# Two attentions of a hybrid decoder layer as flat sequences of steps, with their projections dealt out between the steps; input norm and latents in one block

## The chip, the core and the metric

The kernel runs on one core of a Trainium2 chip. TensorE (PE in the rows) multiplies, VectorE (DVE) and ScalarE (ACT) do elementwise work, GpSimd (POOL) makes masks and issues indirect transfers, SyncE (SP) issues most transfers. The engines run side by side and wait for each other through semaphores. The metric is the device time in microseconds (us) of one launch, median of several runs; lower is better.

## The reference

One decoder layer for 1024 tokens of width 1024, all in float32. What matters here is the mixer part:

```python
h = rmsnorm(x, norm_mix)
q_a, kv_a, dq, dk, dv, gates = split(h @ w_in)
# first mixer (MLA): 8 heads, query and key of 64 + 32 (rotary), value of 64
q = rmsnorm(q_a) @ w_q_b;  kv = rmsnorm(c_kv) @ w_kv_b      # latents of rank 256 and 128
p = softmax(causal(q_nope @ k_nope + q_rope @ k_rope) * scale);  y_mla = p @ v_mla
# second mixer (differential): 4 heads, two queries and two keys of 64 each, value of 128
p0, p1 = softmax(causal(q_c @ k_c * scale + bias[t5_bucket]))  for c in (0, 1)
y_diff = rmsnorm((p0 - lam * p1) @ v_d) * (1 - lambda_init)
x = x + (sigmoid(g_mla) * (y_mla @ w_up_mla) + sigmoid(g_diff) * (y_diff @ w_up_diff)) @ w_out
x = x + moe_ffn(rmsnorm(x))          # top 4 of 32 experts
```

After it comes the final norm. The experts take more than half of the time and are not touched.

## The kernel before

The program is a row of blocks (`nc.Block`). Inside a block each engine has its own list of instructions and meets the others by semaphores; at the end of a block all engines meet. The blocks are `stage_norm`, `stage_latents`, `stage_mla`, `stage_diff`, `stage_merge`, `stage_out`, `stage_route`, `stage_experts`. The change touches the first four.

- `stage_norm` (L230): x comes in 8 tiles of 128 tokens through four buffers. ScalarE sums squares and takes the root (L273, L276), VectorE scales (L296, L298), TensorE transposes (L288), VectorE applies the gain while it moves the tile out of PSUM into `ht` (L306), which holds h transposed. VectorE starts when all five gain vectors have landed (L268).
- `stage_latents` (L310): SyncE and ScalarE issue the loads of weights and small tables at its start. TensorE makes three latent tiles of 128 channels (L403), sums their squares with a matrix of ones (L415), makes the rotary key and the same with halves swapped (L422: two passes of 32 columns), then eight value tiles of the second mixer (L432, 8 products each), eight of the first (L438), and turns the bias table (L443). VectorE meanwhile makes the arguments of sine and cosine, one reciprocal of 2048 columns (L496), and moves the value tiles out of PSUM (L511).
- `stage_mla` (L640): a loop over four pairs of heads. A pass begins with the pair's projections (L684: rotary and plain queries, 8 products of 512 columns; L688: keys, 2 products), which VectorE and ScalarE move to SBUF (L753 to L757, L807, L810). Then come 16 steps, one for each head and tile of 128 queries. A step on TensorE is `score` (L700) of the next step, `turn` (L713, transposes of the probabilities) of this one, `apply` (L724, probabilities times values) of the one before. VectorE adds the mask and takes the row maximum (L768, L770), ScalarE does the exponential (L816); both copy the turned probabilities (L777, L822); VectorE scales the result (L782, L784). Query tile i sees i + 1 key tiles, so steps grow with i from 0 to 7.
- `stage_diff` (L854): a loop over four heads. A pass begins with 32 products of 512 columns (L893), copied by ScalarE (L1024) and VectorE (L961). Then come 8 steps with two score halves each (L908), bias and maximum (L973, L976), exponential (L1031), `combine` (L981 to L987), `turn` (L920), copies (L994, L1044), `apply` (L930), result and its squares (L998, L1037). Each score half has one pair of PSUM banks: `score` of the next step waits for the exponential of this one.

`either` (L530) reads a flag that tells whether positions are one apart, and each engine then takes one of two versions of the work; with these inputs it is the short, causal one. Instructions in a loop pass are written once; in the projections of a float32 product one `matmul` leaves two MATMUL records.

## Time and profile before

| | us |
|---|---|
| median of 3 runs | 2996.05 |
| lowest, highest | 2992.53, 2996.17 |
| time of the profiled execution | 3004.51 |
| its span | 3003.0 |
| granted TensorE clock over the span | 0.95 of full speed |
| TensorE busy | 2808.7 (94%) |
| VectorE busy | 1480.1 (49%) |
| ScalarE busy | 1033.4 (34%) |

The profiled execution takes 8.5 us more than the median. The time falls into stretches: input norm to 28.9 us, latents 29.4 to 186, first mixer 191 to 462, second mixer 469 to 761, merge to 1063, output projection, norm and routing to about 1264, experts to the end. In a row of a timeline the first number is the start and the second the length; what stands in brackets is how long the engine sat idle before and who released it. In a row of a table by stretches the first number after the stretch is its length, then busy time and instructions of each engine, then the granted clock of TensorE (1.00 is 2.4 GHz, 0.50 is 1.2 GHz), share and rate of the transfers.

### The profile page before, as it was taken

How to read it: one execution, taken by the hardware profiler on the slowest of the kernel's cores; microseconds unless marked ns; L12 is line 12 of the kernel's file. 1: busy time of each engine (PE TensorE's matmuls, PEld its weight loads, DVE VectorE, ACT ScalarE, POOL GpSimd, SP SyncE). 2: the span in 40 equal slices, each digit the busy share in tenths (PEclk: the TensorE clock that was granted, in tenths of full speed). 3: DMA queues.
4: the chain of work that ended last, by engine and by line, in shares of the span. 5: the costliest groups of instructions: out<-in, count | busy, mean ns of one | idle time of the engine just before them, and what ended most of it. 6: DMA issues, size and time to landing. Idle time of an engine off the chain costs nothing.

```text
span 3003.0 us, 47092 instructions
## 1 busy us (share of the span) xinstructions
PE 2808.7 (94%) x16548; PEld 2275.4 (76%) x16549; DVE 1480.1 (49%) x2566; ACT 1033.4 (34%) x1610; POOL 293.7 (10%) x308
## 2 busy tenths in 40 slices
PE   6988888888899999799999999999999999999995
PEld 3346664544566645489999999999899999999995
DVE  4334443444411114666666666666345554444554
ACT  2013332222311012145555555554233333333333
POOL 0000000000000012301111111111111111111111
PEclk9988888889999999599999999999999999999997
DMA  4000001000211153566676766666899999999995
GB/s 129 0 10 5 4 0 29 14 14 0 63 42 42 42 180 50 184 202 195 205 222 210 220 198 218 201 216 217 265 338 344 338 339 342 341 341 343 346 337 179
DMA packets 425339, 522.88 MB, mean 174 GB/s; under 512 B 29428, under 2 KB 336280, under 8 KB 425256
## 3 DMA queue, kind: packets, MB, share of 16 engines
q1 hardware_dynamic: 402504, 464.05, 47.6%
q0 software_dynamic: 18432, 57.20, 7.8%
q10 hardware_dynamic: 4352, 0.98, 0.2%
q8 instruction: 29, 0.48, 0.1%
q14 instruction: 22, 0.18, 0.0%
HBM read 482.23 MB, written 39.95 MB: 174 GB/s over the span
## 4 chain that ended last, share of the span: by engine, by line
PE 56%; issue 0%; DMA 0%; DVE 0%; ACT 0%; SPq 0%; POOLq 0%; POOL 0%; ACTq 0%
PE banks L1814 20%; PE banks L1824 19%; PE banks L1865 16%; PE banks L1806 1%; DVE arena L2108 0%; DMA arena<-acc_rows 0%; DMA acc_rows<-arena,rows 0%; ACT parts L1909 0%; DVE parts L2029 0%; SPq L1746 0%; ACT arena L2001 0%; ACT parts L1936 0%; ACT arena L1980 0%; DVE stat L2106 0%; POOLq L1772 0%
## 5 line engine op out<-in xcount | busy, mean ns | idle before, releaser
L1814 PEld LDWEIGHTS banks<-arena 128*128 128x128 f32 x5376 | 604.9, 192 | 8.2 <-issue 6.6
L1814 PE MATMUL banks<-arena 128*128 128x128 f32 x5376 | 605.2, 275 | 6.2 <-issue 6.2
L1824 PE MATMUL banks<-parts 128*128 128x256 f32 x4608 | 558.0, 284 | 7.1 <-issue 4.0
L1824 PEld LDWEIGHTS banks<-parts 128*128 128x128 f32 x4608 | 557.3, 193 | 8.7 <-issue 4.4
L1865 PE MATMUL banks<-parts 128*128 128x512 f32 x2160 | 498.3, 391 | 0.0
L1865 PEld LDWEIGHTS banks<-parts 128*128 128x128 f32 x2160 | 403.0, 188 | 82.1
L2025 DVE TENSOR_TENSOR parts<-arena,parts 128x1024 fp32r<-128x1024 f32 x264 | 315.3, 1222 | 128.3 <-ACT parts L1929 127.8
L2048 DVE TENSOR_SCALAR arena<-banks,arena 128x128 f32<-128x128 f32 (+1 forms) x528 | 181.4, 393 | 335.4 <-PE banks L1814 335.4
L2029 DVE TENSOR_TENSOR parts<-arena,parts 128x1024 fp32r<-128x1024 f32 x192 | 233.8, 1223 | 197.0 <-ACT parts L1936 195.7
L1929 ACT ACTIVATE parts<-arena 128x1024 fp32r<-128x1024 f32 x264 | 269.7, 1054 | 88.4 <-PE banks L1865 44.9
L1936 ACT ACTIVATE parts<-arena 128x1024 fp32r<-128x1024 f32 x192 | 201.1, 1053 | 178.0 <-PE banks L1824 117.7
L1136 PE MATMUL banks<-parts 128*128 128x512 f32 x768 | 184.3, 399 | 4.3 <-ACT parts L1156 4.3
L1136 PEld LDWEIGHTS banks<-parts 128*128 128x128 f32 x768 | 145.1, 189 | 41.5 <-issue 12.2
L1957 ACT ACTIVATE parts<-arena 128x256 fp32r<-128x256 f32 (+1 forms) x132 | 65.4, 496 | 260.3 <-DVE arena L2056 255.4
L1953 ACT ACTIVATE arena<-arena 128x256 f32<-128x256 f32 (+1 forms) x132 | 65.3, 495 | 235.9 <-DVE arena L2048 235.9
L1332 PE MATMUL banks<-arena 128*128 128x512 f32 x256 | 115.2, 609 | 6.2 <-PEq L1086 3.2
L893 PE MATMUL banks<-arena,arena 128*128 128x512 f32 x256 | 112.6, 601 | 7.4 <-issue 7.4
L1791 POOL COPY rows<-entries 128x2 int32 x33 | 5.9, 177 | 1156.3 <-ACT arena L1980 1156.3
L1766 POOL DMA_INDIRECT acc_rows<-arena,rows x66 | 109.3, 1657 | 66.2 <-issue 66.2
L1211 DVE TENSOR_TENSOR arena<-banks,arena 128x512 f32<-128x512 f32 x32 | 20.6, 686 | 189.8 <-ACT arena L1167 189.8
L1128 PE MATMUL banks<-arena 128*128 128x512 f32 x256 | 112.5, 592 | 1.5 <-DVE arena L1191 1.5
L893 PEld LDWEIGHTS banks<-arena,arena 128*128 128x128 f32 x256 | 49.1, 193 | 68.0 <-issue 68.0
(287 smaller groups left out, 2674.4 us busy)
## 6 DMA issues: line engine op xcount, KB each, us to landing
arena<-in_w SPq DMA_DIRECT2D x264, 1024.0 KB, 7.6
arena<-in_w SPq DMA_DIRECT2D x66, 2048.0 KB, 12.7
arena<-in_w_in SPq DMA_DIRECT2D x27, 512.0 KB, 5.0
arena<-in_x SPq DMA_DIRECT2D x16, 512.0 KB, 4.4
h_rows<-arena POOLq DMA_DIRECT2D x10, 512.0 KB, 7.5
acc_rows<-arena SPq DMA_DIRECT2D x8, 512.0 KB, 4.3
arena<-acc_rows SPq DMA_DIRECT2D x8, 512.0 KB, 7.7
out<-arena SPq DMA_DIRECT2D x8, 512.0 KB, 5.7
```

The lines of the kernel that those rows point to most:

```text
L893: last = nc.tensor.matmul(bank(g, 2 * s + c), wst[:, s, k, :], ht[:, k, c * HALF:(c + 1) * HALF], start=(k == 0), stop=(k == KT - 1))
L1128: nc.tensor.matmul(bank(g, 4 * h + b), w[s][b][:, k, :], yt[:, k0 + k, cols], start=(k == 0), stop=(k == 3))
L1136: last = nc.tensor.matmul(bank(g, 4 * h + b), w_parts[:, s, c, b, k, :], part[:, k, cols], start=(k == 0 and c == 0 and part is h_hi), sto ...
L1332: last = nc.tensor.matmul(bank(g, 2 * (t % 2) + h), merged[:, k, t * P:(t + 1) * P], w_out[:, k, h * HALF:(h + 1) * HALF], start=(k == 0), ...
L1814: last = nc.tensor.matmul(bank(g, 2 * (c % 2) + s)[:, a * JOB:a * JOB + P], w1[c][:, s, k, a * P:(a + 1) * P], xt[:, k, 0:P], start=(k == ...
L1824: last = nc.tensor.matmul(bank(g, 2 * (c % 2) + s)[:, a * JOB:(a + 1) * JOB], first_part[p][:, y, k, :], x[:, k, :], start=(k == 0 and y = ...
L1865: last = nc.tensor.matmul(bank(g, 2 * c + h), x[:, f, rows], second_part(q, wide)[:, y, a, :], start=(f == 0 and x is act_hi and y == 0), ...
L1929: nc.scalar.activation(second_part(q, wide)[:, 0], piece_of(q), ACT.Copy).then_inc(w_hi_ready, 1)
L1936: nc.scalar.activation(first_part[p][:, 0], first_of(p), ACT.Copy).then_inc(v_hi_ready.sem, 1)
L2025: nc.vector.tensor_tensor(part[:, 1], piece_of(q), part[:, 0], ALU.subtract).then_inc(w_lo_ready, 1)
L2029: nc.vector.tensor_tensor(first_part[p][:, 1], first_of(p), first_part[p][:, 0], ALU.subtract).then_inc(v_lo_ready.sem, 1)
L2048: nc.vector.tensor_scalar(dst[:, a, 0:w], bank(g, 2 * (c % 2) + s)[:, a * JOB:a * JOB + w], b1_t[:, bass.ds(expert, 1), s * FT + 2 * c + a ...
```

## The change

`stage_norm` and `stage_latents` become one block, `stage_front`. x gets a buffer for each tile; the gain vectors other than `norm_mix` and the small tables move to GpSimd's queue; weights are issued right behind x. The products of the first latent tile's first half stand between the last three transposes. The rotary key and its swapped form are one pass of 64 columns (16 products for 32). Three value tiles of the second mixer are made there (`DV_EARLY`); five are left.

`stage_mla` has no loop over pairs: 128 steps in a row. `side_plan` deals out "units" between `score` and `turn`: the next pair's projections as six units (rotary, plain, keys, for each half of the tokens) in the steps of the pair's second head, and the five value tiles, 3 + 3 + 2 products in the first three steps of each pair (and once more in the last). All of them use PSUM bank 7, so `apply` has bank 6 alone. A unit's first product waits until the unit before it is out of the bank (`wait_taken`); VectorE takes rotary units, ScalarE the others. The results go to a second set of buffers.

`stage_diff` has no loop over heads: 32 steps. A unit is one 512-token half of a head's keys or queries, 8 products in bank 7. Two units stand ahead; the others follow at 4 products a step (8 in step 0), up to step 26. ScalarE copies a unit as fp32r (`high`: 4 copies for keys, 2 for queries), VectorE subtracts that copy from the product to get the rest (`low`, two instructions), and only then does the bank come free. The scores are two fp32r products in place of one float32 product: high and low part of the query stacked on 128 rows times the high key, and high query times low key on 64 rows.

```diff
 def stage_front(g, io):
...
+            for t in range(5):
+                turn(t)
+            pe.wait_ge(w_ready[0], 16)
+            for t, ks in ((5, range(0, 3)), (6, range(3, 6)), (7, range(6, 8))):
+                turn(t)
+                latent(0, 0, ks)
+            pe.wait_ge(ht_ready, TT)
+            latent(0, 1, range(KT)).then_inc(projected, 1)
...
-            for swapped, b in ((0, 6), (1, 4)):
-                for h in range(2):
-                    for k in range(KT):
-                        last = nc.tensor.matmul(bank(g, b + h)[NOPE:HEAD_QK, :], wst[:, 3, k, swapped * ROPE:(swapped + 1) * ROPE],
+            for h in range(2):
+                for k in range(KT):
+                    last = nc.tensor.matmul(bank(g, 6 + h)[NOPE:P, :], wst[:, 3, k, 0:2 * ROPE],
...
 def stage_mla(g, io):
...
-                with pe.Fori(0, MLA_HEADS // 2) as hp:
...
+                    for n, k in fill[u]:
+                        side(n, k)
+                    if u == MLA_STEPS - 1:
+                        apply(u - 1)
+                    turn(u)
...
+                def wait_taken(n):
+
+                    pe.wait_ge(rot_steps, 2 * rotated(n))
+                    pe.wait_ge(side_taken, n - rotated(n))
...
 def stage_diff(g, io):
...
+                    if k == 0:
+                        pe.wait_ge(g.w_head[h % 3], 64 if h == 3 else 32)
+                        if n >= ahead:
+                            pe.wait_ge(lo_made, n)
...
-                                last = nc.tensor.matmul(bank(g, 2 * c + a // HALF)[:, 0:n], q_t[rows, i * P:(i + 1) * P],
-                                                        k_t[rows, a:a + n], start=True, stop=True)
+                        nc.tensor.matmul(out, q_c[c][:, cols], k_c[h % 2][c][:, a:a + n], start=True, stop=False)
+                        last = nc.tensor.matmul(out, q_c[c][rows, cols], k_low[h % 2][rows, a:a + n], start=False, stop=True)
...
+                    half = len(fill[u]) // 2
+                    if u + 1 < DIFF_STEPS:
+                        score(u + 1, 0)
+                    for n, k in fill[u][:half]:
+                        project(n, k)
+                    if u + 1 < DIFF_STEPS:
+                        score(u + 1, 1)
+                    for n, k in fill[u][half:]:
+                        project(n, k)
...
+                    if kind == KEY:
+                        k0, k1 = k_c[h % 2]
+                        for out, rows in ((k0[first, cols], first), (k0[second, cols], first), (k1[second, cols], second), (k1[first, cols], second)):
+                            last = nc.scalar.activation(out, src[rows], ACT.Copy)
+                    else:
+                        for c0, rows in ((0, first), (1, second)):
+                            last = nc.scalar.activation(q_c[c0][rows, cols], src[rows], ACT.Copy, scale=DIFF_SCALE)
+                    last.then_inc(hi_made, 1)
```

Where instructions stand now, on TensorE from the latents' rotary key on. Before (L415 sums of squares of the last latent, L422 rotary key, L432 value tiles of the second mixer, L438 of the first, L443 bias):

```order
L415 MATMUL banks<-arena_0,ones 128x512 x2
L422 MATMUL banks<-arena_0,arena_1 32x512 x32
L432 MATMUL banks<-arena_0 128x512 x64
L438 MATMUL banks<-arena_1 128x512 x8
L443 MATMUL banks<-arena_1,flip 128x256 x4
```

After (L387, L393, L401, L409, L414 are the same five):

```order
L387 MATMUL banks<-arena_0,ones 128x512 x2
L393 MATMUL banks<-arena_0,arena_2 64x512 x16
L401 MATMUL banks<-arena_1,arena_0 128x512 x24
L409 MATMUL banks<-arena_1,arena_2 128x512 x8
L414 MATMUL banks<-arena_1,flip 128x256 x4
```

Of 96 products of these two kinds 40 are left. TensorE around the start of a pair's second head in the first mixer, after the change (L740 is `score`, L724 a rotary unit, L753 `turn`, L764 `apply`):

```order
L740 MATMUL banks<-arena_1 128x256
L724 MATMUL banks<-arena_0 128x512 x2
L753 MATMUL banks<-ident,arena_0 128x128
L764 MATMUL banks<-arena_0 128x64 x8
L740 MATMUL banks<-arena_1 128x384
L724 MATMUL banks<-arena_0 128x512 x2
L753 MATMUL banks<-ident,arena_0 128x128 x2
L764 MATMUL banks<-arena_0 128x64
```

The rotary units of the next pair stand in steps whose own work is small. Before, the same eight products of both query kinds stood in a row ahead of the pair's first score (L684, keys L688, `score` L700):

```order
L684 MATMUL banks<-arena_0 128x512 x8
L688 MATMUL banks<-arena_1,arena_0 128x512 x2
L690 ISA
L691 ISA
L700 MATMUL banks<-arena_1 128x128
L700 MATMUL banks<-arena_1 128x256
```

TensorE in the second mixer, before: a whole head's projections, then its first steps (L908 `score`, L920 `turn`):

```order
L893 MATMUL banks<-arena_0,arena_1 128x512 x32
L896 REGISTER_ALU
L908 MATMUL banks<-arena_1 128x128 x2
L904 REGISTER_ALU
L908 MATMUL banks<-arena_1 128x256
L904 REGISTER_ALU
L908 MATMUL banks<-arena_1 128x256
L913 ISA
L920 MATMUL banks<-ident,arena_0 128x128
```

After, one step in the middle of a head (L1021 and L1022 are the two fp32r products of a score half, L1005 the unit's products, L1034 `turn`, L1045 `apply`):

```order
L1021 MATMUL banks<-parts_3 128x512
L1022 MATMUL banks<-parts_3 128x512
L1021 MATMUL banks<-parts_3 128x128
L1022 MATMUL banks<-parts_3 128x128
L1005 MATMUL banks<-arena_0,arena_1 128x512 x2
L1021 MATMUL banks<-parts_3 128x512
L1022 MATMUL banks<-parts_3 128x512
L1021 MATMUL banks<-parts_3 128x128
L1022 MATMUL banks<-parts_3 128x128
L1005 MATMUL banks<-arena_0,arena_1 128x512 x2
L1034 MATMUL banks<-ident,arena_0 128x128 x4
L1045 MATMUL banks<-arena_1,arena_0 128x128 x3
```

Each half of the scores is followed by two products of a unit, and each projection waits in TensorE's queue for its bank. On ScalarE the copies of a unit come after the step's probabilities are copied (L1185 exponential, L1199 copy of turned probabilities, L1174 `high` of keys, L1192 squares):

```order
L1185 ACTIVATE arena_0,den<-banks,den 128x768 x2
L1199 ACTIVATE arena_0<-banks 128x512
L1174 ACTIVATE parts_3<-banks 64x512 x4
L1192 ACTIVATE arena_0,ssq<-arena_1 128x128
L1185 ACTIVATE arena_0,den<-banks,den 128x896 x2
```

Before, ScalarE had one copy of 1024 columns for a head's queries (L1024), ahead of the steps.

## Rows read from the trace of the kernel before

**Rows 1.** The page, chain that ended last: shares of the span by line.

```profile
PE banks L1814 20%; PE banks L1824 19%; PE banks L1865 16%; PE banks L1806 1%; DVE arena L2108 0%; DMA arena<-acc_rows 0%; DMA acc_rows<-arena,rows 0%; ACT parts L1909 0%; DVE parts L2029 0%; SPq L1746 0%; ACT arena L2001 0%; ACT parts L1936 0%; ACT arena L1980 0%; DVE stat L2106 0%; POOLq L1772 0%
```

**Rows 2.** Table by stretches: length, busy us of each engine, clock, transfers.

```profile
33.30:48.70 15.40, 15.40 (x33) 6.61 (x33) 4.74 (x6) 0.00 (x0) 0.00 (x0) 0.90 0.97 254
48.70:91.20 42.50, 35.79 (x79) 14.87 (x78) 17.81 (x22) 3.26 (x6) 0.00 (x0) 0.96 0.06 18
91.20:118.80 27.60, 27.60 (x65) 6.96 (x64) 16.45 (x4) 5.50 (x5) 0.00 (x0) 1.00 0.00 1
118.80:182.70 63.90, 63.81 (x153) 28.80 (x152) 15.47 (x21) 0.00 (x0) 0.00 (x0) 1.00 0.03 5
182.70:191.00 8.30, 0.00 (x0) 0.00 (x0) 2.89 (x6) 1.28 (x1) 1.04 (x4) 0.73 0.02 6
191.00:205.30 14.30, 11.66 (x20) 4.80 (x20) 4.88 (x4) 4.08 (x4) 0.00 (x0) 0.80 0.05 9
205.30:260.00 54.70, 49.40 (x264) 37.88 (x265) 26.18 (x70) 21.24 (x49) 0.00 (x0) 0.83 0.03 5
260.00:329.00 69.00, 61.10 (x287) 42.91 (x287) 31.60 (x77) 25.31 (x53) 0.00 (x0) 0.82 0.03 5
469.20:500.30 31.10, 29.71 (x64) 12.86 (x65) 1.23 (x1) 1.02 (x1) 0.00 (x0) 0.94 0.01 2
617.00:690.00 73.00, 63.72 (x225) 35.39 (x224) 32.70 (x70) 20.62 (x59) 0.00 (x0) 0.91 0.06 14
```

**Rows 3.** Groups by line: value tiles (float32), merge products (fp32r); two and one record each.

```profile
L1136 PE MATMUL banks<-parts 128*128 128x512 f32 x768 | 184.3, 399 | 4.3 <-ACT parts L1156 4.3
...
L432 PE MATMUL banks<-arena 128*128 128x512 f32 x128 | 55.2, 593 | 0.0
```

**Rows 4.** Timeline of the norm's first and last tile and the first latent.

```profile
10.42 0.16 DVE L296 RECIPROCAL stat<-stat 128x1 f32<-128x1 f32 x1 [10.31 <-DMA gain_ffn<-in_norm_ffn]
...
27.65 1.23 DVE L306 TENSOR_TENSOR arena<-banks,gain_mix 128x1024 f32<-128x1024 f32 x1 [0.73 <-PE banks L288]
...
33.27 15.50 PE L403 MATMUL banks<-arena,arena 128*128 128x512 f32 x32 [5.66 <-DMA arena<-in_w_in]
```

**Rows 5.** Timeline of TensorE, second head of the first pair.

```profile
228.51 0.44 PE L700 MATMUL banks<-arena 96*128 96x128 f32 x2
230.09 1.06 PE L713 MATMUL banks<-ident,arena 128*128 128x128 f32 x8 [1.13 <-ACT arena L822]
...
249.77 1.45 PE L724 MATMUL banks<-arena 128*128 x12
...
256.56 3.68 PE L724 MATMUL banks<-arena 128*128 x16 [0.78 <-DVE arena L777]
```

**Rows 6.** Timeline of VectorE and TensorE, last steps of a head, second mixer.

```profile
524.55 0.17 DVE L981 RECIPROCAL den<-den 128x2 f32<-128x2 f32 x1 [0.86 <-ACT arena L1031]
...
530.38 0.17 DVE L981 RECIPROCAL den<-den 128x2 f32<-128x2 f32 x1 [0.83 <-ACT arena L1031]
...
536.72 0.17 DVE L981 RECIPROCAL den<-den 128x2 f32<-128x2 f32 x1 [0.81 <-ACT arena L1031]
...
537.41 2.71 PE L930 MATMUL banks<-arena,arena 128*128 x14 [2.78 <-ACT arena L1044]
```

**Rows 7.** Groups by line: moving 512 columns out of PSUM on ScalarE and VectorE.

```profile
L1167 ACT ACTIVATE arena<-banks 128x512 f32<-128x512 f32 x32 | 17.4, 594 | 206.9 <-PE banks L1136 206.9
...
L511 DVE COPY arena<-banks 128x512 f32<-128x512 f32 x16 | 11.1, 692 | 47.1 <-PE banks L432 45.8 <-PE banks L438 1.3
```

**Rows 8.** Table by stretches of 5 us at the end of two heads, second mixer.

```profile
605.00:610.00 5.00, 2.23 (x19) 2.07 (x18) 4.09 (x7) 3.18 (x7) 0.00 (x0) 0.98 0.00 0
610.00:615.00 5.00, 4.22 (x23) 3.98 (x23) 1.97 (x4) 0.89 (x3) 0.00 (x0) 0.68 0.00 0
...
680.00:685.00 5.00, 2.27 (x20) 2.30 (x21) 3.16 (x6) 2.38 (x7) 0.00 (x0) 1.00 0.00 0
685.00:690.00 5.00, 4.22 (x25) 3.01 (x24) 1.30 (x3) 1.69 (x7) 0.00 (x0) 1.00 0.00 0
```

More of the change, by code:

```diff
@@ L645, in stage_mla @@
     neg_max, total, inv = g.den[:, 0:16], g.den[:, 16:32], g.den[:, 32:48]
+    units, fill, done, ready = side_plan()
+    rotated = lambda n: sum(kind == ROTATE for kind, p, half in units[:n])
+    unit_bank = lambda n: bank(g, (2, 3, 0, 1, 4, 5)[n] if n < len(PAIR_UNITS) else 7)
     with nc.Block() as block:
@@ L739, in _ @@
+                apply(MLA_STEPS - 1)
             either(g, pe, attend)
@@ new lines, in score @@
+                def score(u, c):
+                    h, i = divmod(u, TT)
+                    keys, s = (end(i) + 1) * P, 2 * u + c
+                    if c == 0:
+                        pe.wait_ge(lo_made, units_before(u, general))
+                    if s >= 2:
+                        pe.wait_ge(exped, s - 1)
+                    rows, cols = (first, second)[c], slice(i * P, (i + 1) * P)
+                    for a in range(0, keys, HALF):
+                        n = min(HALF, keys - a)
+                        out = bank(g, 2 * c + a // HALF)[:, 0:n]
+                        nc.tensor.matmul(out, q_c[c][:, cols], k_c[h % 2][c][:, a:a + n], start=True, stop=False)
+                        last = nc.tensor.matmul(out, q_c[c][rows, cols], k_low[h % 2][rows, a:a + n], start=False, stop=True)
+                    last.then_inc(scored, 1)
@@ L945, in _ @@
+                apply(DIFF_STEPS - 1)
             either(g, pe, attend)
@@ new lines, in attend @@
+                for n in range(ahead):
+                    low(n)
+                row_max(0)
+                combine(0)
+                for u in range(DIFF_STEPS):
+                    if u + 1 < DIFF_STEPS:
+                        row_max(u + 1)
+                    copy_late(u)
+                    if u + 1 < DIFF_STEPS:
+                        combine(u + 1)
+                    for n in done[u]:
+                        low(n)
+                    if u >= 1:
+                        store_y(u - 1)
@@ new lines, in exp @@
+                def exp(u):
+                    keys = (end(u % TT) + 1) * P
+                    for c in range(2):
+                        s = 2 * u + c
+                        act.wait_ge(max_known, s + 1)
+                        nc.scalar.activation(prob[:, s % 4, 0:keys], bank(g, 2 * c, 2)[:, 0:keys], ACT.Exp,
+                                             bias=neg_max[:, s % HALVES:s % HALVES + 1],
+                                             accum_out=total[:, s % HALVES:s % HALVES + 1]).then_inc(exped, 1)
@@ L1056, in _ @@
+                for n in range(ahead):
+                    high(n)
+                exp(0)
+                for u in range(DIFF_STEPS):
+                    if u + 1 < DIFF_STEPS:
+                        exp(u + 1)
+                    copy_early(u)
+                    for n in done[u]:
+                        high(n)
+                    if u >= 2:
+                        square(u - 2)
+                square(DIFF_STEPS - 2)
+                square(DIFF_STEPS - 1)
             either(g, act, attend)
```

798 lines of the change are left out of this document (426 added, 372 removed).

## The prediction

> **What bounds the kernel now.** I read the chain that ended last first: it lies on TensorE and, as far back as it goes, in the experts, which the change leaves alone [rows 1]. Whatever the blocks ahead give up moves the end by the same amount. So the question is how long the first four blocks last, and the table by stretches answers which limit holds in each [rows 2]. From 91.2 to 182.7 us TensorE is busy without a gap at full clock: a product less is time less. From 182.7 to 191.0 it does nothing: end of block, flag, branch. In the attentions it is busy 49.4 of 54.7 us, but the clock is 0.83: about a third of the stretch runs at 1.2 GHz. VectorE is busy 26 of 54.7 there and about half of a head in the second mixer. So TensorE bounds the attentions as well, and it has little idle time for other work to fill. The gain has to come from fewer products, from the pair and head boundaries, and from the clock. My prices are 0.863 us for a float32 product of 512 columns (55.2 us for 64) and 0.240 us for an fp32r one (184.3 us for 768) [rows 3].
>
> **Front block.** (a) VectorE starts the norm at 10.42 us, when the last gain vector lands, then needs 17.2 us to its last tile at 27.65 [rows 4], and is the bound at 2.0 us a tile. With one gain to wait for, the first root sets the start; I take 1.4 us earlier. The products dealt between the last three transposes (8 x 0.863 = 6.9 us) delay the last tiles: transposes of tile 5 from about 20.4, then 2.6 us of products, 1.1 of transposes, 2.6, 1.1, and the gain of the last tile 1.2: ht is complete near 30.2. The second half follows, 8 x 0.863, so the first latent ends at 37.6. Before it ended at 48.7: 5.66 us waiting for weights issued only after the block's end, then 15.5 us [rows 4]. Gain 11.1, bounds 5 (if the ten small loads on GpSimd's queue land only after 38 us, since the bias row and VectorE's chain wait for them) and 14. (b) From 48.7 to 91.2 the order is the same: 0. (c) The rotary key: 16 products for 32, 13.8 of the 27.6 us [rows 2]. What is late next there is VectorE's key work, which waits behind the long reciprocal, but TensorE's three value tiles (20.7 us) cover it. (d) Five value tiles leave: 5 x 8 x 0.863 = 34.5 us. Sum 59 us; the 8.3 us of block end stay. They come back in the next block in part.
>
> **First mixer.** Before: 14.3 us of projections and copies, then 54.7 us for 16 steps [rows 2], four times, less the last boundary: 191.0 to 461.8, 270.8 us. Within a pair the first head takes 23.2 us (205.3 to 228.5). Clock 0.83 over 54.7 us means 18.6 us at half speed; I put 12 of them at the pair's start and the rest at its end. The second at full clock takes 22.7 (228.51 to 251.2), with TensorE idle 2.2 (1.13 of it in one place), and ends at 260.2 because the last steps have nothing behind them [rows 5]. After: start 13.2 (copies by halves overlap a little better), first head 23.2, six heads of 22.7 = 136.2, last head with its tail 31.7: 204.3 us. Dealt into it: three pairs of 10 products (25.9) and 40 products of the value tiles (34.5): 60.4. Of it the idle time hides at most 2.2 a head, and I take 15 in all. Against that stand the handovers of bank 7: a rotary unit is taken by VectorE in about 4 x 0.69 us, a plain one by ScalarE in 2 x 0.594 [rows 7], while TensorE has turn, apply and the next score to do, about 1.3 us or more. I take 5 us for 18 units (0 to 15). Sum 204.3 + 60.4 - 15 + 5 = 254.7, gain 16. Bounds: nothing hidden and 15 of handovers, a loss of 9; 20 hidden and no handover waits, a gain of 26. The two extra copies of the rotary key on VectorE lie in the wait for the branch.
>
> **Second mixer.** Before: 469.2 to 761.0, 291.8 us. TensorE's work for a head: 63.7 us busy of 73.0 at clock 0.91 [rows 2]. Clock 0.91 means 13 us at half speed, so 57.1 us at full. Projections are 32 x 0.863 = 27.6; scores are 9216 columns, 18 x 0.863 = 15.5; 14.0 are left for turn and apply. After, scores are 36 x 0.240 = 8.6, so steps cost 22.6, and with 4 products in each of 8 steps (27.6) a head costs 50.2 us. VectorE needs 5.8 and 6.3 us for the heaviest steps [rows 6], and `low` adds 2 x 0.69 every second step: 6.5 and 7.0 on average against about 7 and 7.5 on TensorE. TensorE stays the bound, closely.
>
> The new wait decides. A unit's last product stands ahead of `turn`. ScalarE copies the turned probabilities (up to 0.6), then does `high` (4 x 0.594 for keys, 2 x 0.594 for queries), VectorE does `low` (1.4). Only then may TensorE start the next unit, and meanwhile it has only `apply` and one score half (0.5 to 2.3 us). Behind the waiting product stand the other score half and `turn` on TensorE, and so row maximum and exponential on VectorE and ScalarE. Going through the four unit places of a head with these durations I get waits of 3.0 (keys, tile 4), 2.5 (queries, tile 6), 2.0 (keys, tile 0) and 2.1 (queries, tile 2): 9.6 a head, 28.7 for three.
>
> Sum: 16.0 for two units ahead (half of the 29.7 us of [rows 2], with its cold start), 2.9 until their `low` is done, 23.2 for steps 0 to 2 (16 products, 3.6 of steps, 5.8 of two handovers), 3 x 50.2 + 28.7 = 179.3 for steps 3 to 26, 27 for the last five without a fill (tiles 5 to 7 took 524.55 to 545.5, bound by VectorE [rows 6]): 248.4. Then the clock. After an idle time of about 2.8 us it fell in one place and not in another that looks alike: 0.68 behind 605 to 610, 1.00 behind 680 to 685 [rows 8]. Fourteen waits of 2 to 4 us, half of them followed by a stretch at 1.2 GHz that costs some 2 us: 15 us. Total 263.4, gain 28. Bounds: clock never falls 43; a fall behind each wait, 4 us each, a loss of 13.
>
> The clock rows decide over the rule: the Trainium skill, "TensorE: Matmul & The Clock Gate", section on psum-queue depth-cycling, says that small idle times from handing banks round make the clock swing between its two levels. By that rule every handover in both mixers costs clock; the trace agrees at 610 and not at 685. Taken strictly it gives the slower end of the range, which is the second rival.
>
> **The sum.** 59 + 16 + 28 = 103 us. Against the profiled 3004.5 that gives 2901.5; the median of the runs is 8.5 lower, so I forecast 2893.
>
> **Rivals.** (1) The handover waits don't show, since copies run ahead of what I walked through, and the clock stays up: 28.7 + 5.8 + 15 come back, 2844. For it: my walk puts full durations one behind the other; against: ScalarE's order puts `high` behind the copy of turned probabilities, and bank 7 is the only one. Chance 0.12. (2) The waits pull the clock down each time. Before, the first steps of a pair ran some 12 us at 1.2 GHz, a loss of 6, after TensorE had idled 2.6 of the 14.3 us ahead [rows 2]. With 3 to 6 us at each of 14 handovers the second mixer loses 42 to 84 in place of 15: 2920 to 2962, middle 2941. For it: row 610; against: dealt products keep TensorE loaded right behind the wait. Chance 0.18. (3) Slower than before: the same in both mixers. The steps ask for about 390 us of TensorE's work at full clock; each us of it that runs at 1.2 GHz costs one more. Here 118 us would have to be lost beyond the 15, a third of the work of both mixers at half clock. With 6 us at each of 14 handovers and 3 at each of 18 in the first mixer it is 69 + 54 = 123: 3016. Chance 0.03. (4) The change doesn't hide what it deals out: TensorE is busy anyway, so value tiles moved from the front come back one to one and the pair boundaries give little: first mixer at its bound, a loss of 9 for a gain of 16, and small loads late, 6 more: 2924. Chance 0.12. The forecast with its neighbourhood has 0.55.
>
> **Range and chances.** 2855 to 2942: it holds the forecast, most of (4), half of (2), and leaves out (1), (3) and the upper half of (2). A difference of 0.2%, 6 us, is about what a measurement can tell. Faster 0.96, same 0.01, slower 0.03.
>
> **What the changed profile would show.** Right: the first latent ends near 38 us; TensorE's last product of the front ends near 124; the first mixer takes about 255 us from its first product, with few idle times over 1 us and a clock above 0.95; the second takes about 263 us, with TensorE waiting for `low` (L1086 and following on VectorE) in total some 30 us before L1005, and short stretches at 0.5. Wrong: that wait missing; VectorE without idle time in the second mixer (then it is the bound); the norm stretched past 31 us by the dealt products or by loads; the experts' stretch changed in length, which could only come from other counts of tokens per expert through the rounding of the scores.

## The result: 46 us faster where 103 were forecast

The median is 2949.95 us (four runs, 2944.53 to 2955.22) against 2996.11 us of the kernel before on the same chip. The ratio is 0.9846, with a 95% interval from 0.9833 to 0.986: 46 us less, or 1.5%. The prediction said 2893.0, range 2855 to 2942: the direction holds, the time lies outside the range.

The profiled execution took 2944.53 us, its span 2943.1. The profiled execution of before stood 8.5 us above its median, this one 5.4 below, so the two traces differ by 60 us. A second series of the kernel after, shown below, tells which number is meant: the traces explain where the time sits, the gain is 46. Of all executions below one, of `e4_both`, took 6062.8 us for a reason that no run shows, and it is left out.

The page, chain that ended last, shares of the span by line, answers [rows 1]:

```profile
PE banks L1973 20%; PE banks L1983 19%; PE banks L2024 17%; PE banks L1965 1%; DMA arena<-acc_rows 0%; DMA acc_rows<-arena,rows 0%; SPq L1905 0%; ACT parts L2068 0%; DVE arena L2267 0%; DVE parts L2188 0%; ACT arena L2160 0%; ACT parts L2095 0%; ACT arena L2139 0%; POOLq L1931 0%; POOL acc_rows L1925 0%
```

It is the same chain through the experts. From its first piece (at 1264.57 us before, at 1203.77 now) to the end it was 1738.4 us and is 1739.3: what the early stages give, the end takes over. The table by stretches (columns as in [rows 2]) has front, first mixer, boundary and second mixer one under the other:

```profile
0.00:134.50 134.50, 102.60 (x279) 47.12 (x280) 71.24 (x80) 22.24 (x38) 9.28 (x29) 0.97 0.26 75
134.50:394.00 259.50, 237.66 (x1216) 160.13 (x1216) 130.67 (x323) 103.09 (x231) 0.00 (x0) 0.97 0.04 9
394.00:399.30 5.30, 0.00 (x0) 0.00 (x0) 0.06 (x1) 0.00 (x0) 0.00 (x0) 0.50 1.05 265
399.30:701.10 301.80, 259.77 (x880) 142.03 (x881) 150.97 (x304) 105.48 (x273) 0.00 (x0) 0.90 0.03 7
```

The two mixers before, in the same columns:

```profile
191.00:462.00 271.00, 239.14 (x1136) 166.98 (x1136) 125.68 (x303) 99.97 (x211) 0.00 (x0) 0.84 0.02 4
...
469.20:761.00 291.80, 254.23 (x880) 143.27 (x880) 129.10 (x276) 80.88 (x228) 0.00 (x0) 0.89 0.04 11
```

| stretch | before | after | gain | forecast |
|---|---|---|---|---|
| front, to the first mixer's first product | 191.0 | 134.5 | 56.5 | 59 |
| first mixer | 271.0 | 259.5 | 11.5 | 16 |
| boundary | 7.2 | 5.3 | 1.9 | 0 |
| second mixer | 291.8 | 301.8 | -10.0 | 28 |

So the miss is one stage. The second mixer was to become 28 us shorter and became 10 longer. In the same stretch before, TensorE was busy 254.2 us, VectorE 129.1, ScalarE 80.9, at clock 0.89. Now the added copies are there (VectorE 151.0, ScalarE 105.5), but TensorE is busy longer, 259.8 us, although 9216 columns a head went from float32 to fp32r.

What TensorE waits for in that stage, total us, times, longest:

```profile
PE banks L1021 <- DVE parts L1097: 20.4, 8, 2.7
PE banks L1005 <- DVE parts L1093: 15.4, 7, 3.6
```

Both end with `low`, but they are two kinds of wait. The seven before L1005, the unit's product, are handovers of bank 7. The eight before L1021, the first product of a score, are waits for the operand: `score` waits until the `low` of the unit that it reads is done, at the start of the stage and then after each query unit. Apart from the start, the text ahead of the prediction, and the prediction, speak of the bank alone; by the program a second bank would leave these eight as they are. And this is a piece of it, TensorE in the middle of the first head (start, length, waits in brackets):

```profile
448.63 0.50 PE L1021 MATMUL banks<-parts 128*128 128x512 f32 x1 [2.64 <-DVE parts L1097]
449.06 0.50 PE L1022 MATMUL banks<-parts 64*128 64x512 f32 x1
449.50 0.33 PE L1021 MATMUL banks<-parts 128*128 128x128 f32 x1
449.76 0.32 PE L1022 MATMUL banks<-parts 64*128 64x128 f32 x1
450.01 3.46 PE L1005 MATMUL banks<-arena,arena 128*128 128x512 f32 x4
452.48 1.42 PE L1021 MATMUL banks<-parts 128*128 128x512 f32 x1
```

Read the starts, not the lengths (lengths overlap). From 448.63 to 449.06 and on to 449.50 a product of 512 columns takes 0.43 us; the one of 128 columns takes 0.26. The line through both is 0.45 ns a column and 0.20 us for each product, whatever its size. It is not the clock: at half clock the columns would cost double and nothing would be added (in `e1_full_rows` below, at 0.50, the same two products take 0.43 and 0.11 us), and here the clock is 1.00. The forecast's price was 0.240 us, from the merge, where it is unchanged (185.7 us for 768, [rows 3]):

```profile
L1295 PE MATMUL banks<-parts 128*128 128x512 f32 x768 | 185.7, 401 | 4.2 <-DVE parts L1359 4.2
```

A piece from another step, at clock 1.00 too, shows the weight loads (PEld) beside the products:

```profile
465.86 0.49 PE L1022 MATMUL banks<-parts 64*128 64x512 f32 x1
466.29 0.44 PE L1021 MATMUL banks<-parts 128*128 128x384 f32 x1
...
465.86 0.18 PEld L1022 LDWEIGHTS banks<-parts 64*128 64x128 f32 x1 [0.24 <-issue]
466.29 0.19 PEld L1021 LDWEIGHTS banks<-parts 128*128 128x128 f32 x1 [0.24 <-issue]
```

Each load starts with its own product, not ahead of it, and 0.24 us lie between two loads.

In the first piece, the last two lines show the second cost: from 450.01 to 452.48 two float32 products take 2.47 us where 1.73 is the price at full clock. The table of 5 us, columns as in [rows 8], shows the clock around two waits of 2.64 us (they end at 448.63 and 661.97):

```profile
445.00:450.00 5.00, 2.36 (x12) 1.48 (x10) 2.87 (x6) 2.27 (x7) 0.00 (x0) 1.00 0.78 196
450.00:455.00 5.00, 5.00 (x10) 2.10 (x10) 1.38 (x3) 0.89 (x2) 0.00 (x0) 0.66 0.06 14
...
665.00:670.00 5.00, 5.00 (x17) 3.45 (x16) 2.98 (x6) 2.54 (x7) 0.00 (x0) 0.50 0.01 2
...
680.00:685.00 5.00, 5.00 (x20) 4.11 (x19) 2.95 (x7) 2.94 (x7) 0.00 (x0) 0.50 0.00 0
```

Behind 448.63 the clock fell to 1.2 GHz for some 3 us, behind 661.97 for more than 20 us although TensorE was busy without a gap. Read in steps of 2 us, the stage shows a fall behind each of the nine waits of 2.38 us or more, and behind one of the six of 1.83 to 2.08 us: ten falls in fifteen waits. In long stretches it comes to this:

```profile
417.60:660.00 242.40, 210.45 (x720) 112.34 (x720) 125.60 (x259) 87.86 (x229) 0.00 (x0) 0.93 0.02 5
660.00:701.10 41.10, 33.73 (x128) 23.04 (x129) 22.62 (x41) 14.08 (x39) 0.00 (x0) 0.71 0.00 1
```

The nine short falls cost some 17 us of TensorE's work ((1 - 0.93) x 242.4), the one long fall at the end 12. The second series of this kernel has 0.93 and 0.71 in the same two stretches.

### The profile page after: what moved, and what is told of

Read it like the earlier page. It is cut to its first block, busy times and chain, and to the rows that moved or that the text cites. A ratio compares the mean times of both kernels' runs of the same rounds, so it can differ in the third digit from the quotient of the medians.

```text
span 2943.1 us, 46180 instructions
## 1 busy us (share of the span) xinstructions
PE 2762.7 (94%) x16516; PEld 2249.2 (76%) x16517; DVE 1504.2 (51%) x2607; ACT 1057.2 (36%) x1670; POOL 299.4 (10%) x318
## 4 chain that ended last, share of the span: by engine, by line
PE 57%; DMA 1%; issue 0%; ACT 0%; DVE 0%; SPq 0%; POOLq 0%; POOL 0%; ACTq 0%
PE banks L1973 20%; PE banks L1983 19%; PE banks L2024 17%; PE banks L1965 1%; DMA arena<-acc_rows 0%; DMA acc_rows<-arena,rows 0%; SPq L1905 0%; ACT parts L2068 0%; DVE arena L2267 0%; DVE parts L2188 0%; ACT arena L2160 0%; ACT parts L2095 0%; ACT arena L2139 0%; POOLq L1931 0%; POOL acc_rows L1925 0%
## 5 line engine op out<-in xcount | busy, mean ns | idle before, releaser
L1973 PEld LDWEIGHTS banks<-arena 128*128 128x128 f32 x5376 | 605.0, 192 | 8.3 <-issue 6.7
L1295 PE MATMUL banks<-parts 128*128 128x512 f32 x768 | 185.7, 401 | 4.2 <-DVE parts L1359 4.2
L1185 ACT ACTIVATE arena<-banks,den 128x128 f32<-128x128 f32 (+7 forms) x64 | 47.4, 741 | 165.0 <-DVE den L1114 164.9
L1491 PEld LDWEIGHTS banks<-arena 128*128 128x128 f32 x256 | 49.1, 194 | 65.6 <-issue 62.7
```

What stands on the lines that cost most here:

```text
L1295: last = nc.tensor.matmul(bank(g, 4 * h + b), w_parts[:, s, c, b, k, :], part[:, k, cols], start=(k == 0 and c == 0 and part is h_hi), sto ...
L1491: last = nc.tensor.matmul(bank(g, 2 * (t % 2) + h), merged[:, k, t * P:(t + 1) * P], w_out[:, k, h * HALF:(h + 1) * HALF], start=(k == 0), ...
L1973: last = nc.tensor.matmul(bank(g, 2 * (c % 2) + s)[:, a * JOB:a * JOB + P], w1[c][:, s, k, a * P:(a + 1) * P], xt[:, k, 0:P], start=(k == ...
```

## The experiments

Questions: is the dear product due to the change of row count between neighbours (the first product of a score loads 128 rows of weights, the second 64)? What do the handovers cost with their clock? What does the dealing hide? All kernels are the kernel after with an edit. Each median stands beside runs of before on the same chip; the ratio is what compares the kernels, and gains below are differences of ratios. By the intervals each gain is good to some 10 us. Code is shown cut; three dots stand for what is left out.

| kernel | median us | ratio to before, 95% interval |
|---|---|---|
| after (first series) | 2949.95 | 0.9846 (0.9833 to 0.986) |
| after_again | 2949.35 | 0.9845 (0.9826 to 0.9864) |
| e1_full_rows | 2921.32 | 0.9746 (0.9712 to 0.978) |
| e2_float32_scores | 2907.67 | 0.9695 (0.9661 to 0.9728) |
| e3_whole_units | 2940.89 | 0.981 (0.9777 to 0.9843) |
| e4_both | 2929.01 | 0.9768 (0.9736 to 0.9799) |
| e5_values_early | 2959.34 | 0.9858 (0.9832 to 0.9883) |
| e6_rows64 | 2940.03 | 0.9792 (0.9767 to 0.9817) |
| e7_no_low | 2911.95 | 0.9693 (0.9665 to 0.9721) |
| e8_full_no_low | 2878.78 | 0.9597 (0.9571 to 0.9623) |
| e10_padded_float32 | 2893.77 | 0.9651 (0.9631 to 0.9672) |
| e9_one_fp32r | 2854.93 | 0.9523 (0.9501 to 0.9544) |

For the second mixer I split each trace in three. Length and TensorE's busy time are read from the table by stretches, from the first product of the mixer to the first transposes of the merge. Clock loss is (1 - clock) x length, since a us at half speed does half a us of work (the clock has two digits, so about 1.5 us of error). Work is busy time less that loss. These are estimates from rows, not rows.

| second mixer | length | idle | clock loss | work at full clock |
|---|---|---|---|---|
| before | 291.8 | 37.6 | 32.1 | 222.1 |
| forecast for after | 263.4 | 47.6 | 15 | 200.8 |
| after | 301.8 | 42.0 | 30.2 | 229.6 |
| e1_full_rows | 274.7 | 50.4 | 27.5 | 196.9 |
| e6_rows64 | 298.3 | 46.7 | 38.8 | 212.8 |
| e7_no_low | 265.0 | 20.5 | 13.3 | 231.2 |
| e8_full_no_low | 233.6 | 29.5 | 4.7 | 199.4 |
| e3_whole_units | 294.9 | 34.1 | 29.5 | 231.3 |
| e2_float32_scores | 259.7 | 13.3 | 7.8 | 238.6 |
| e10_padded_float32 | 248.2 | 18.3 | 7.4 | 222.5 |
| e9_one_fp32r | 209.4 | 23.7 | 4.2 | 181.5 |

### The second product over all 128 rows

```diff
-                        last = nc.tensor.matmul(out, q_c[c][rows, cols], k_low[h % 2][rows, a:a + n], start=False, stop=True)
+                        last = nc.tensor.matmul(out, q_c[c][:, cols], k_low[h % 2][:, a:a + n], start=False, stop=True)
```

The same number of products and columns; the sum takes in products of low parts that don't belong to it.

> The changed kernel with one edit: the second fp32r product of a score half runs over all 128 rows instead of 64 (it adds the product of the two low parts of the other component, far below the accuracy kept). In the changed kernel an fp32r product of 512 columns is followed by the next 0.43 us later in the scores, but 0.22 us later in the merge. Theory A: what costs the extra 0.2 us is the change between 128-row and 64-row weights, which keeps a weight load from running beside the product before it. Then the distance falls to about 0.22 us, the 192 score products give back some 0.2 us each, 38 us of TensorE's work, and the time is 2950 less 25 to 38: 2912 to 2925. Theory B: it is the short groups (two products, then another PSUM bank). Then the distance stays at 0.43 us and the time at 2950.

Measured: 0.9746, that is 30 us less than after. TensorE, same place of the head as above:

```profile
446.75 0.59 PE L1021 MATMUL banks<-parts 128*128 128x512 f32 x1 [2.64 <-DVE parts L1097]
447.14 0.63 PE L1022 MATMUL banks<-parts 128*128 128x512 f32 x1
447.57 0.31 PE L1021 MATMUL banks<-parts 128*128 128x128 f32 x1
447.68 0.42 PE L1022 MATMUL banks<-parts 128*128 128x128 f32 x1
...
451.16 0.40 PE L1022 MATMUL banks<-parts 128*128 128x512 f32 x1
451.40 0.22 PE L1021 MATMUL banks<-parts 128*128 128x128 f32 x1
451.46 0.27 PE L1022 MATMUL banks<-parts 128*128 128x128 f32 x1
...
451.17 0.19 PEld L1021 LDWEIGHTS banks<-parts 128*128 128x128 f32 x1
451.40 0.19 PEld L1022 LDWEIGHTS banks<-parts 128*128 128x128 f32 x1
```

The clock was 0.50 from 447.1 to 449. Away from that, a product takes 0.24 us for 512 columns (451.16 to 451.40) and 0.06 for 128. The weights of the product at 451.40 are loaded from 451.17 on, beside the product before. Work falls by 32.7 us (192 products at 0.2 would be 38) to 196.9, some 4 us below the forecast's 200.8. The price was right for neighbours of equal height.

### The first product on 64 rows too

```diff
-                        nc.tensor.matmul(out, q_c[c][:, cols], k_c[h % 2][c][:, a:a + n], start=True, stop=False)
+                        nc.tensor.matmul(out, q_c[c][rows, cols], k_c[h % 2][c][rows, a:a + n], start=True, stop=False)
```

> The kernel after with the first fp32r product of a score also on 64 rows: the queries' low part is left out of the computation, the number of products and all copies stay. If the dear products come from the change between weights of 128 and of 64 rows, products follow each other after 0.22 us and the time falls to about 2922, like the kernel with full rows. Rival: weights of 64 rows are dear by themselves in fp32r; then 0.43 us and 2950 remain.

```profile
450.00 0.40 PE L1022 MATMUL banks<-parts 64*128 64x512 f32 x1
450.24 0.22 PE L1021 MATMUL banks<-parts 64*128 64x128 f32 x1
450.30 0.27 PE L1022 MATMUL banks<-parts 64*128 64x128 f32 x1
450.50 1.93 PE L1005 MATMUL banks<-arena,arena 128*128 128x512 f32 x3
```

Inside the scores products are cheap again (0.24 and 0.06 us), so weights of 64 rows are not dear by themselves; it is the step between 64 and 128 rows that costs (the unit's product comes 0.20 us behind the last one, 450.30 to 450.50, in e1 0.11). At these edges, between fp32r and float32, the difference is 0.09 us and not 0.20. Theory B of the first run, short groups, falls too, since the groups are as short as before. The total did not follow my expectation, 0.9792 in place of some 0.975: work is 212.8 us, 15.9 more than in e1, which the edges of the 64 score groups could explain (no run has them alone), and the clock loss rose to 38.8 us. Why the clock is lower here than in e1, with nearly the same waits for `low` (37.0 and 38.9 us), no run tells apart.

### Float32 scores

```diff
-                        nc.tensor.matmul(out, q_c[c][:, cols], k_c[h % 2][c][:, a:a + n], start=True, stop=False)
-                        last = nc.tensor.matmul(out, q_c[c][rows, cols], k_low[h % 2][rows, a:a + n], start=False, stop=True)
+                        last = nc.tensor.matmul(out, q_t[rows, cols], k_t[h % 2][rows, a:a + n], start=True, stop=True)
```

`low` and `high` go; ScalarE copies a unit once and the bank is free.

> The changed kernel with the split scores undone: one float32 product on 64 rows as before, ScalarE copies a projection unit with one instruction, VectorE has no low parts to make; the flat steps and dealt units stay. If the split scores cost more on TensorE than float32 ones (about 18 us a head against 15.5) and their copies make the handover waits of the unit bank (33 us in the trace of the changed kernel), the second mixer falls from 302 to about 262 us and the time to 2912 (2905 to 2925). Rival: the waits come from the one bank whatever the copies cost: then only the 10 us of products come back, 2940.

Measured 0.9695, inside the expected range. This is the change without its fp32r part, and it is 45 us better than with it: the split into two products, meant as the cheaper form, costs 45 us. Work is 238.6 us, though, 9 more than after and 16 more than before, whose products it shares. In before the scores stood beside each other; dealt out, each half has products of 128 rows on both sides. That the steps between 64 and 128 rows are the reason is what the next run tests.

### Float32 scores over 128 rows

The edit against the kernel with float32 scores, cut:

```diff
-                        last = nc.tensor.matmul(out, q_t[rows, cols], k_t[h % 2][rows, a:a + n], start=True, stop=True)
+                        last = nc.tensor.matmul(out, q_c[c][:, cols], k_t[h % 2][:, a:a + n], start=True, stop=True)
...
+                for z in (q_c[0][second], q_c[1][first]):
+                    nc.vector.memset(z, 0.0).then_inc(hi_made, 1)
```

> The kernel with float32 scores, with the queries in two tiles that hold zeros in the other component's 64 rows: a score product then takes all 128 rows of queries and of keys and gives the same sum. If a product between others on 128 rows loses 0.20 us because it has 64 rows (0.63 us for 256 columns, half of 0.863 is 0.43), 96 score products give back 19 us: 2886 (2882 to 2893). Rival: the loss belongs to any product that stands alone between others; then 2905 remains.

Measured 0.9651, 13 us better than e2, 19 expected; 16.1 us of work went. Idle time rose from 13.3 to 18.3 us: ScalarE now copies a query unit into two tiles with two instructions, and the waits for its copies grew from 3.2 to 8.8 us. First e2, then e10, TensorE in a step with 256 keys:

```profile
484.10 0.70 PE L1020 MATMUL banks<-flat 64*128 64x256 f32 x2
484.73 1.98 PE L1004 MATMUL banks<-arena,arena 128*128 128x512 f32 x4
486.64 0.70 PE L1020 MATMUL banks<-flat 64*128 64x256 f32 x2
```

```profile
482.93 0.60 PE L1021 MATMUL banks<-flat 128*128 128x256 f32 x2
483.36 1.88 PE L1005 MATMUL banks<-arena,arena 128*128 128x512 f32 x4
485.08 0.59 PE L1021 MATMUL banks<-flat 128*128 128x256 f32 x2
```

A score product of 256 columns takes 0.63 us in e2 and 0.43 in e10, exactly half of 0.863; the two products behind it take 1.91 and 1.72. So each step in height, down or up, costs 0.2 us between these float32 products, as it does between fp32r ones. Rows of zeros cost TensorE nothing and save it; the second copy is what they cost elsewhere. The sum is the reference's sum, and this is the faster of the two kernels here that round nothing: 104 us below before, 58 below after.

### The handover without low parts

The low parts are filled with zeros once, at the start of the stage; the scores are then computed from high parts alone.

```diff
-                for n in range(ahead):
-                    low(n)
...
-                    for n in done[u]:
-                        low(n)
...
-                    last.then_inc(hi_made, 1)
+                    last.then_inc(lo_made, 1)
```

> The kernel after without VectorE's low parts: they stay zero, so the scores are computed from high parts alone, and bank 7 comes free right after ScalarE's copies. Products and ScalarE's copies stay. Each handover is 1.4 us shorter: 14 x 1.4 = 20 us and some clock, so 2920 to 2930, with products still 0.43 us apart. Rival (the handover is the whole difference to the kernel with float32 scores): 2908 or below.

Measured 0.9693, 46 us less than after; I had expected 20 to 30. The waits:

```profile
PE banks L1021 <- ACT parts L1163: 7.9, 8, 1.4
PE banks L1005 <- ACT parts L1160: 5.4, 7, 2.2
```

They sum to 13.3 us, 22.5 less than after, as worked out (14 x 1.4 = 20, and the one at the start). The clock loss falls from 30.2 to 13.3, 17 more us, which I had put at "some". The work is the same, 231.2. So a us of wait for `low` cost about 1.75 us. From e1 to e8, the same edit on cheaper products, 21.9 us of waits went and 22.8 of clock loss: 2.0. The rival, that the handover is everything, gets its number but not its reason: the products are as dear as before (446.45 to 446.89), and e8 takes that cost away on top.

```profile
446.45 0.51 PE L1021 MATMUL banks<-parts 128*128 128x512 f32 x1 [1.21 <-ACT parts L1163]
446.89 0.49 PE L1022 MATMUL banks<-parts 64*128 64x512 f32 x1
```

### Both edits

e1's edit and e7's.

> Both edits: second product over all 128 rows (which adds products of low parts that don't belong to the scores, here zeros), no low parts made. If product price and handover are two separate costs, their gains add: 2950 - 29 - 25 = 2896 (2888 to 2905), below the kernel with float32 scores at 2908. Rival: with cheaper products TensorE comes sooner to a handover that still takes ScalarE's 2.4 us, and half of the gain is lost: 2908 to 2915.

Measured 0.9597: 75 us below after, where e1 alone gives 30 and e7 alone 46. The two gains add, 76 against 75, as closely as the intervals tell, and the rival of half a gain (2908 to 2915) is refuted. My own range, 2888 to 2905, was missed too, since the gain of e7 was put too low. With 2878.78 us it came out under the forecast's 2893. Its computation leaves the low parts out.

### One fp32r product

The e10 kernel with queries and keys held as fp32r: half the products of e8, two copies or one for a unit.

> The kernel e10 with the queries and keys rounded to fp32r: one fp32r product per 512 keys over 128 rows, the low parts are left out of the scores. Copies and handovers as in e10, so the difference to e10 is the price of the score products alone: 18 columns groups of 512 a head, 0.863 against 0.24 us, 4 heads: 45 us, 2841 (2835 to 2855). Rival: with so little work of TensorE in a step the softmax chain on VectorE and ScalarE sets the pace (about 7 us for the heaviest step), and half of the gain turns into waits: 2860 to 2870.

Measured 2854.93, 0.9523: 38 us less than e10 where 45 were expected, at the edge of the expected range (2835 to 2855) and below the rival's. Work fell by 41.0 us, and idle time rose from 18.3 to 23.7. It is the fastest kernel here, at the price of rounded scores; whether a layer may pay that is not for a profile to say.

### A unit in one step

```diff
-        for u in range(3, 27):
-            fill[u] = [(4 + (u - 3) // 2, 4 * ((u - 3) % 2) + k) for k in range(4)]
+        for u in range(3, 27, 2):
+            fill[u] = [(4 + (u - 3) // 2, k) for k in range(8)]
```

> The changed kernel with another dealing in the second mixer: from step 3 on a unit's 8 products stand in one step and the next step has none, so the bank has a whole step to come free. If the handover is what TensorE waits for, the 12 waits of 1.8 to 2.6 us behind VectorE's low parts vanish: 27 us less, 2923, and no wait of that kind in the trace. Rival: a step without a fill is bound by VectorE and ScalarE (4 to 6 us of VectorE's work), so the waits come back at transposes and scores: 2940 to 2955.

Measured 0.981, 11 us less than after; the rival's range holds. Of the 35.8 us of waits for `low` 8.9 are left, three waits, but TensorE now waits elsewhere:

```profile
PE banks L1045 <- DVE arena L1138: 14.7, 11, 2.9
PE banks L1021 <- ACT arena L1185: 9.1, 10, 1.3
```

The first is the wait of `apply` until VectorE has taken the last result out of bank 6, the only one left to it; the second is the wait of `score` for the exponential. That a step without a unit has too little work to cover VectorE's and ScalarE's chain, and that one with eight products holds it up, fits both rows, but no run shows it apart from the single bank. The clock loss stayed, 29.5.

> Full rows and whole units together. If both theories hold and TensorE stays the bound, the gains add: 2950 - 33 - 27 = 2890. If VectorE becomes the bound in the heavier steps (6 to 7 us of work a step with low parts), part of it is lost: 2900 to 2915. If rows don't matter: as the kernel with whole units alone.

With e1's edit added it is 0.9768, no better than e1 alone (0.9746), and 2929.01 us lies above all the times that I had expected if rows matter (2890 to 2915). The shorter the scores, the less there is to cover a step without a unit. No trace of this kernel can be set beside the others, so this reading is an argument.

### All value tiles in the front

```diff
-DV_EARLY = 3
+DV_EARLY = 8
...
-        for first in (0, 3) if p == MLA_HEADS // 2 - 1 else (0,):
+        for first in ():
```

> The kernel after with all eight value tiles of the second mixer made in the front block, none dealt out between the steps of the first mixer. The front block grows by 5 x 8 x 0.863 = 34.5 us. Prediction's step: idle time of TensorE in the first mixer hides at most 15 of the 60 us that are dealt out, so its share of these 34.5 us is about 9; the first mixer then shortens by about 26 us and the whole is 9 us slower than the kernel after, 2955 to 2962. Rival (nothing is hidden, TensorE is busy anyway): 2948 to 2952. Rival (dealt products are hidden in full): 2984.

TensorE's first product of each mixer in this kernel:

```profile
170.23 2.07 PE L726 MATMUL banks<-arena 128*128 128x512 f32 x2 [9.11 <-issue]
...
408.32 2.07 PE L1007 MATMUL banks<-arena 128*128 128x512 f32 x2 [7.03 <-issue]
```

The first mixer starts 35.8 us later than in the kernel after (134.47), the second 9.0 later (399.34). So of the work that is dealt out some 27 us return in the first mixer and about 9 are hidden, as forecast. TensorE's idle time in the first mixer, 25.6 us here against 21.8, holds 4 of the 9; the rest is 1.5 us of clock loss (0.96 against 0.97), 1.3 by which the front grew beyond 34.5, and rounding. The medians are less sharp: the ratios differ by 0.0012, 4 us, inside their intervals; "nothing hidden" is refuted by the trace alone.

### The kernel after, once more

> The kernel after once more beside these, to place its median: its gain was 46 us in medians and 60 us between the two profiled executions. If the profile of before was a slow draw, the ratio stays at 0.984 to 0.986 and this kernel's profiled time lies within 6 us of its median; if the first comparison was off, the ratio comes out near 0.980.

0.9845 and a profiled span of 2945.7 us: the first case holds. Forecast and result are to be compared in medians, and the profiled execution of before lay 8.5 us above its median. The 14 us between the two ways of counting are how the two profiled executions lie to their medians (8.5 and 5.4); the runs do not tell in which stage.

## Why the prediction was wrong, step by step

- **What bounds.** Right: the chain in the experts is unchanged and the gain of the early stages passes through; the experts' stretch kept its length.
- **Front block, 59 for 56.5.** The norm was to start 1.4 us earlier than 10.42 [rows 4] and starts 1.4 later:

```profile
7.65 1.28 ACT L329 ACT_TABLE_LOAD   x1 [7.52 <-DMA arena<-in_x]
...
11.81 0.16 DVE L423 RECIPROCAL stat<-stat 128x1 f32<-128x1 f32 x1 [11.69 <-ACT stat L331]
...
39.52 0.80 PE L374 MATMUL banks<-arena 32*4 32x383 f32 x2
```

  ScalarE now waits for tiles in pairs (`x_in[t // 2]`), a wait that the kernel shows and my working missed: the first pair is there at 7.52 us, where the first tile was there at 4.73 before. No run has single waits, so how much of the delay this makes is open. The last tile's gain ends at 32.3, forecast 30.2 and past the 31 that I had named as a sign of being wrong. The first latent ends at 39.5, forecast 37.6. TensorE's last product of the front ends at 125.4, forecast 124. The terms for the rotary key and the value tiles held.
- **First mixer, 254.7 for 259.5.** The handovers cost 4.8 us (waits before L724), forecast 5. The dealing hides about 9 of 34.5 us, as e5 shows, in line with 15 of 60.4. The clock is 0.97, not 1: (1 - 0.97) x 259.5 = 7.8 us, and my heads at 22.7 us had none. That covers the difference. Split like the second mixer, the stage shows where its gain came from: before, 31.9 us idle, 43.4 of clock loss, 195.8 of work; after, 21.8, 7.8 and 229.9. The work grew by 34.1 us, the value tiles' 34.5. The clock paid for them: its loss fell by 35.6 us, idle time by 10.1.
- **Second mixer, 263.4 for 301.8: here the prediction fell.** By the table, three terms make up the 38.4 us. (1) The price of a score product, 0.240 us for 512 columns from [rows 3], so 8.6 us a head: measured 0.43, and 28.8 us more work than forecast for the four heads. The step that failed is carrying a price from the merge, where all neighbours have 128 rows, to a place where 128 and 64 alternate; e1, e6 and e8 show it, with work at 196.9, 212.8 and 199.4 us. Since float32 scores were not dearer than that, the step that was to bring 28 us brought none. (2) The clock: 15 us forecast, 30.2 measured, which e7 ties to the waits. I had half of the waits followed by a loss of 2 us; from 417.6 to 660 us it was nine of fourteen waits and 17 us, so the term was nearly right there. What it had no place for is the long fall of the last 41.1 us, 12 us. (3) Idle time 47.6 forecast, 42.0 measured, 5.6 in the other direction (its forecast is what the sum leaves beside 4 x 50.2 us of work and the 15). The wait on `low` itself was right: 14 handovers, 33 us, forecast 34.5. But half of them stand before L1021, since a query unit ends just in time for the score that needs it: a wait for the operand, where my walk had only the bank.
- **Clock rows against the rule.** I took row 610 and row 685 as even odds, over the rule of the Trainium skill, "TensorE: Matmul & The Clock Gate", section on psum-queue depth-cycling. In the kernel after, with waits for `low` of 1.8 to 3.6 us, ten of fifteen were followed by a fall and the loss was 30.2; in e7, where the longest was 2.2 us, the loss was 13.3; in e8, longest 2.4, it was 4.7. So the trace agrees with the rule in more cases than I had granted, and disagrees for a third of the waits.
- **Rivals.** None names the dear product. Rival (2) had the right sign, a clock loss for the second mixer of 42 to 84 us; measured 30. Its time, 2920 to 2962, holds the result by luck, for a reason that covers 15 of the 38 us. Rival (4), 2924, put the missing gain into the first mixer, where e5 shows none missing.
- **The range** took its bounds from waits and clock, and gave the product price no bound at all, though no row showed an fp32r product between weights of unequal height.

## What to carry to other kernels

Before taking a product's price from another stage, compare the heights of the weights of its neighbours, not only type and columns; where heights alternate, fill the short operand up with rows of zeros, and count the copies that this takes. A result that two engines must take one after the other before TensorE goes on costs more than its wait, because the clock goes with it: here 1.75 to 2.0 us for each us of wait. Ask of each such wait whether it is for the bank or for the operand: a second bank helps only the first kind (no run here has one). When a change makes one form cheaper and adds copies to get it, time it without that form too.

## What the runs showed of the hardware

- A product whose weights have another number of rows than those of the product before (64 against 128) starts 0.2 us later: 0.43 in place of 0.24 us for 512 columns in fp32r, 0.63 in place of 0.43 for 256 columns in float32. It costs the same down and up. 96 rows beside 128 in the first mixer show little of it: 384 columns take 0.70 us there, three quarters of 0.863 is 0.65. The 0.2 us is the length of one weight load (188 to 204 ns a load in the groups by line). The rows of PEld agree: between weights of equal height the load runs beside the product before (451.17, in e1), between unequal ones it starts only with its own product (465.86). So a load that is not hidden is the likely mechanism; why it is not hidden, the traces do not show.
- The Trainium skill, "TensorE: Matmul & The Clock Gate", section on the mechanism of row and column tiling, says in its list of what overlaps that a weight load overlaps running products only when the row group differs; the paragraph above it also allows it for a load into a background buffer. The trace disagrees with the "only" of the list: between weights of equal height on the same 128 rows the load is hidden (451.17, beside the product of 451.16 to 451.40), and where the heights differ it shows. With the background buffer the hidden load agrees, but neither sentence gives the exposed one.
- Behind the last wait of 2.64 us TensorE ran 20 us at 1.2 GHz, busy all the time, while the same wait at 448.63 cost about 3 us of low clock. What differs is that no unit products follow. In e7 the wait at the same place is 1.21 us (it ends at 630.26), and the clock is 0.50 from 635 to 645 all the same, so the length of the wait does not set it. No run here tells what does.
